# A trunk step of two layers: the first layer's modulation, made in the first stage or in part between the projections

## The reference, cut to what matters

```python
mod = silu(c) @ ada_w[l] + ada_b[l]              # 1024 x 6144: six vectors of 1024 for each group
sh1, sc1, g1, sh2, sc2, g2 = jnp.split(mod, 6, axis=-1)
h = _rms(x, norm1_g) * (1 + sc1) + sh1           # needs sh1 and sc1 alone
... = _split_in(h @ p['w_in'])                   # projections: q, k, v of four branches, gates
... four attentions, with head norms and rotary embedding; gates; w_out ...
x = x + g1 * y                                   # needs g1
h2 = _rms(x, norm2_g) * (1 + sc2) + sh2          # sc2, sh2
x = x + g2 * _peer(h2, ...)                      # g2; 16384 experts, top 16 of 8 heads
```

## Time and profile before

| | us |
|---|---|
| median of three timed runs (5416.52 to 5420.11) | 5418.61 |
| the profiled execution | 5413.07 |
| its span | 5411.3 |

### The profile page before, as it was taken

How to read it: one execution, slowest core, us unless ns; L and a number is a source line. 1 busy time by engine, 2 the same in 40 slices (tenths; PEclk the granted TensorE clock), 3 DMA queues, 4 the chain that set the end, 5 groups by cost and what they waited for, 6 DMA issues and landing times.

```text
span 5411.3 us, 68396 instructions
## 1 busy us (share of the span) xinstructions
PE 5099.5 (94%) x25512; PEld 4124.9 (76%) x25512; DVE 3206.5 (59%) x7229; ACT 1676.5 (31%) x2610; POOL 1325.4 (24%) x858
## 2 busy tenths in 40 slices
PE   4979999889999999999989799998899999999999
PEld 1846688677888887888868467877788888788887
DVE  1556411107998995666654763111488998766666
ACT  2325422222333332222232353212233333322222
POOL 1310022214344331111123001213244344211111
PEclk6978999999999999999999799999999999999999
DMA  6200021264877878888831001222367877888886
GB/s 228 71 29 1 11 73 65 74 242 170 270 239 260 281 258 308 289 288 291 293 121 58 15 1 35 68 65 66 131 219 263 280 261 239 316 286 294 291 288 222
DMA packets 349128, 981.98 MB, mean 181 GB/s; under 512 B 31648, under 2 KB 100128, under 8 KB 345504
## 3 DMA queue, kind: packets, MB, share of 16 engines
q1 hardware_dynamic: 215232, 553.19, 31.6%
q0 software_dynamic: 74880, 276.86, 14.6%
q10 hardware_dynamic: 58720, 148.04, 7.0%
HBM read 829.43 MB, written 148.54 MB: 181 GB/s over the span
## 4 chain that ended last, share of the span: by engine, by line
PE 84%; DVE 6%; DMA 3%; ACT 3%; POOL 1%; issue 1%; DVEq 1%; ACTq 0%; POOLq 0%; SPq 0%
PE PS L813 26%; PE PS L773 23%; PE PS L474 15%; PE PS L463 5%; PE PS L795 4%; PE PS L601 3%; PE PS L627 2%; PE PS L464 1%; DVE AR L1183 1%; PE PS L611 1%; POOL HR L1516 1%; PE PS L571 1%; DMA WR<-in_ada 1%; PE PS L761 1%; DVE SM L1222 1%
## 5 line engine op out<-in xcount | busy, mean ns | idle before, releaser
L813 PE MATMUL PS<-HB,VR 128*128 128x512 f32 x6144 | 1397.1, 390 | 17.2 <-DVE HB L1473 17.2
L813 PEld LDWEIGHTS PS<-HB,VR 128*128 128x128 f32 x6144 | 1156.3, 188 | 258.0 <-issue 18.0
L773 PE MATMUL PS<-HR,UR 128*128 128x512 f32 x4128 | 1013.0, 399 | 0.0
L1516 POOL TENSOR_TENSOR UR<-WR,UR 128x1024 fp32r<-128x1024 f32 x212 | 530.6, 2504 | 1838.7 <-ACT UR L995 938.0
L474 PE MATMUL PS<-HR,UR 128*128 128x320 f32 (+1 forms) x5952 | 924.0, 315 | 44.0 <-POOL HR L1516 38.8
L474 PEld LDWEIGHTS PS<-HR,UR 128*128 128x128 f32 x5952 | 888.4, 190 | 69.9 <-issue 47.6
L773 PEld LDWEIGHTS PS<-HR,UR 128*128 128x128 f32 x4128 | 768.2, 190 | 166.9
L1460 DVE TENSOR_TENSOR VR<-HT,VR 128x1024 fp32r<-128x1024 f32 x256 | 313.8, 1226 | 459.7 <-ACT VR L1113 374.4
L1113 ACT CAST VR<-HT 128x1024 fp32r<-128x1024 f32 x256 | 268.8, 1050 | 962.7 <-PE PS L813 960.2
L773 PE MATMUL PS<-HR 128*128 128x512 f32 x2016 | 486.7, 394 | 0.0
L773 PEld LDWEIGHTS PS<-HR 128*128 128x128 f32 x2016 | 372.1, 188 | 73.6
(11 more groups left out here) (183 smaller groups left out, 5975.4 us busy)
## 6 DMA issues: line engine op xcount, KB each, us to landing
WR<-in_uT SPq DMA_DIRECT2D x256, 512.0 KB
HT<-in_vtab SPq DMA_DIRECT2D x256, 512.0 KB, 4.0
activations<-AR ACTq DMA_DIRECT2D x256, 256.0 KB
gates_by_expert<-AR ACTq DMA_DIRECT2D x128, 512.0 KB, 3.5
HW<-activations SPq DMA_DIRECT2D x256, 256.0 KB
WR<-gates_by_expert SPq DMA_DIRECT2D x64, 1024.0 KB
WR<-in_wgate SPq DMA_DIRECT2D x64, 640.0 KB, 3.9
WR<-in_ada SPq DMA_DIRECT2D x24, 1024.0 KB, 4.9
```

What stands on the lines that cost most here:

```text
L773: last = pe.matmul(bank(n % 2), u_part(n, w)[:, c, :], HR[:, h, c, 0:LAT], start=c == 0 and i == 0, stop=c == DC - 1 and i == 2)
L813: last = pe.matmul(bank(d), VR[:, m % 4, w, P * d:P * d + P], HB[:, (m + 1) % 3, h, :], start=m == 0 and i == 0, stop=m == E1 - 1 and i == 2)
L1516: nc.gpsimd.tensor_tensor(dst, src, high.bitcast(F32), ALU.subtract).then_inc(sem_, 1)
```

## The change

The first stage of layer one keeps only the first third of the modulation, 8 steps of 24, and puts each behind one chunk of the norm's sums (`norm_sum`). The ring's numbers follow (`N_FIRST` = 16 blocks instead of 48). The other 16 steps (`rest_step`) run in stage two, two ahead of each of the projections 0 to 7, from two buffers of their own (REST_W, in space that the values and the keys of branch D fill later), and add up in PSUM bank 7. ScalarE copies the rows out at s = 3 and s = 7, TensorE turns them at s = 9, VectorE copies, adds the bias and makes the second scale at s = 10; `values` waits for that copy. GpSimd clears the row buffers at the start of stage two. SP issues the first four loads behind the first four projection blocks and the norm's sums, the others behind blocks 4 to 9. In stage one VectorE now takes the reciprocal before it waits for the turned modulation. Layer two is as before.

```diff
-B_FM = N_ADA
+N_FIRST = N_ADA // SETS
+B_FM = N_FIRST
...
+        REST_W = [VT[:, 0:4, :].rearrange("p a b -> p (a b)"), DKF[:, 0:2 * D]]
+        REST_R = [VT[:, 5, :], DKF[:, 2 * D:2 * D + 512]]
...
@@ SP
-                    with sp.Fori(0, N_ADA // RING) as i:
+                    with sp.Fori(0, N_FIRST // RING) as i:
...
+                def load_rest(step):
+                    if step >= 2:
+                        sp.wait_ge(rest_used, step - 1)
+                    sp.dma_start(REST_W[step % 2].rearrange("p (a t) -> p a t", a=2),
+                                 ada[l, N_FIRST + 2 * step:N_FIRST + 2 * step + 2].rearrange("a b t -> b a t")
+                                 ).then_inc(rest_in[step % 2], 16)
                 for n in range(RING):
                     load(l, B_FM + n, WR[:, (B_FM + n) % RING, 0:D], wfm[l, n])
+                if l == 0:
+                    sp.wait_ge(ss_ready, 1)
+                    for step in range(4):
+                        load_rest(step)
                 sp.wait_ge(hr_ready, l * (2 * DC) + DC)
...
                 for n in range(RING, N_FM):
                     load(l, B_FM + n, WR[:, (B_FM + n) % RING, 0:D], wfm[l, n])
+                    if l == 0 and 2 * n - 3 < 2 * DC:
+                        for step in (2 * n - 4, 2 * n - 3):
+                            load_rest(step)
@@ TensorE
+            def norm_sum(c):
+                pe.wait_ge(sq_ready, c + 1)
+                last = both(cols(0), ones, lambda lo, hi: NSQ[:, c, lo:hi], c == 0, c == DC - 1)
+                if c == DC - 1:
+                    last.then_inc(ss_ready, 1)
...
             def values(l):
                 pe.wait_ge(y_ready, l * NI + N_FM)
+                pe.wait_ge(rest_kept, 1)
...
+                def rest_step(step):
+                    which, c = divmod(step, DC)
+                    pe.wait_ge(rest_in[step % 2], 16 * (step // 2 + 1))
+                    if step == DC:
+                        pe.wait_ge(rest_out, 1)
+                    for j in range(4):
+                        last = pe.matmul(bank(7)[32 * j:32 * j + 2, :], CS[:, 2 * c:2 * c + 2],
+                                         REST_W[step % 2][:, 512 * j:512 * j + 512], start=c == 0, stop=c == DC - 1)
+                    last.then_inc(rest_used, 1)
+
+                def turn_rest():
+                    pe.wait_ge(rest_out, 2)
...
+                    for which in range(2):
+                        for q in range(4):
+                            last = pe.matmul(out[:, which, :, q, :], REST_R[which][:, P * q:P * q + P], pick, start=True, stop=True)
+                    last.then_inc(rest_turned, 1)
-                norm(l, 0)
                 if l == 0:
-                    for which in range(SETS):
-                        for c in range(DC):
-                            modulation(which, c)
-                    for which in range(SETS):
-                        turn_modulation(which)
+                    for c in range(DC):
+                        norm_sum(c)
+                        modulation(0, c)
+                    turn_modulation(0)
+                else:
+                    norm(l, 0)
                 phase_end(pe, l, 0)
                 for s in range(NI + 2):
+                    if l == 0 and s < DC:
+                        rest_step(2 * s)
+                        rest_step(2 * s + 1)
+                    if l == 0 and s == 9:
+                        turn_rest()
@@ ScalarE
+            def rest_rows(which):
+                act.wait_ge(rest_used, DC * (which + 1))
...
+                for j in range(4):
+                    rows = slice(32 * j, 32 * j + 2)
+                    last = nc.scalar.copy(REST_R[which][rows, :], bank(7)[rows, :])
+                last.then_inc(rest_out, 1)
...
-                    for which in range(SETS):
-                        modulation_rows(l, which)
+                    modulation_rows(l, 0)
...
                 for s in range(NI + 1):
+                    if l == 0 and s in (3, 7):
+                        rest_rows(s // 4)
@@ VectorE
                 if l == 0:
-                    dve.wait_ge(ada_turned, SETS)
-                    nc.vector.tensor_copy(NEXT[:, :], MODT)
+                    norm(l, 0)
+                    dve.wait_ge(ada_turned, 1)
+                    nc.vector.tensor_copy(NEXT[:, 0:32], MODT[:, 0:32])
...
                 for s in range(1, NI + 2):
+                    if l == 0 and s == 10:
+                        dve.wait_ge(rest_turned, 1)
+                        nc.vector.tensor_copy(NEXT[:, 32:96], PF[:, 3584:3648]).then_inc(rest_kept, 1)
+                        dve.drain()
+                        nc.vector.tensor_tensor(MD[:, 32:96], NEXT[:, 32:96], GN[:, G_ADAB + 32:G_ADAB + 96], ALU.add)
+                        dve.drain()
+                        nc.vector.scalar_tensor_tensor(SC[:, 1], MD4[:, 4], 1.0, GN[:, G_N2:G_N2 + 16].rearrange("p (c g) -> p c g", c=DC),
+                                                       ALU.add, ALU.mult)
@@ GpSimd
+                if l == 0:
+                    nc.gpsimd.memset(REST_R[0], 0.0)
+                    nc.gpsimd.memset(REST_R[1], 0.0).then_inc(rest_clear, 1)
                 low_h(0)
```

More of the change, by code:

```diff
@@ L69, in loads @@
 def loads(l, n):
-    first = N_ADA if l else 0
-    pairs = 0 if l else sum(m % RING == n % RING for m in range(N_ADA) if m < n)
+    first = N_FIRST if l else 0
+    pairs = 0 if l else sum(m % RING == n % RING for m in range(N_FIRST) if m < n)
     before = loads(l - 1, BLOCKS + n % RING) if l else 0
@@ L78, in block_no @@
 def block_no(l, n):
-    return l * (BLOCKS - N_ADA) + n
+    return l * (BLOCKS - N_FIRST) + n
 SPLIT_NO = {n: i for i, n in enumerate([*range(B_FM, B_DQ), *range(B_GATE, B_WOUT), *range(B_WQ, BLOCKS)])}
@@ L215, in build @@
         shared = a.at
+        DKF = DK.rearrange("p a b -> p (a b)")
+        REST_W = [VT[:, 0:4, :].rearrange("p a b -> p (a b)"), DKF[:, 0:2 * D]]
+        REST_R = [VT[:, 5, :], DKF[:, 2 * D:2 * D + 512]]
         q_ = Arena(AR, shared, AF)
@@ L293, in build @@
         cs_sig = sem("cs_sig")
+        rest_in, rest_used = [sem(f"rest_of_modulation_in{k}") for k in range(2)], sem("rest_of_modulation_used")
+        rest_clear, rest_out, rest_turned, rest_kept = (sem(n) for n in (
+            "rest_rows_cleared", "rest_rows_out", "rest_turned", "rest_kept"))
         next_in, next_used = [sem(f"next_modulation_in{k}") for k in range(3)], sem("next_modulation_used")
@@ L651, in turn_modulation @@
                     last.then_inc(ada_turned, 1)
-                norm(l, 0)
-                if l == 0:
-                    for which in range(SETS):
-                        for c in range(DC):
-                            modulation(which, c)
-                    for which in range(SETS):
-                        turn_modulation(which)
+                def rest_step(step):
[9 more added lines that the diff above has]
+                    pe.wait_ge(rest_out, 2)
+                    out = PF[:, 3584:3648].rearrange("p (s j q g) -> p s j q g", s=2, j=4, q=4)
+                    pick = ident.rearrange("p (j r) -> p j r", j=4)[:, :, 0:2]
+                    for which in range(2):
+                        for q in range(4):
+                            last = pe.matmul(out[:, which, :, q, :], REST_R[which][:, P * q:P * q + P], pick, start=True, stop=True)
+                    last.then_inc(rest_turned, 1)
+                if l == 0:
+                    for c in range(DC):
[4 more added lines that the diff above has]
+                    norm(l, 0)
                 phase_end(pe, l, 0)
                 for s in range(NI + 2):
+                    if l == 0 and s < DC:
[3 more added lines that the diff above has]
+                        turn_rest()
                     if s == N_FM:
@@ L929, in modulation_rows @@
                 last.then_inc(ada_out, 1)
+            def rest_rows(which):
+                act.wait_ge(rest_used, DC * (which + 1))
+                if which == 0:
+                    act.wait_ge(rest_clear, 1)
+                for j in range(4):
+                    rows = slice(32 * j, 32 * j + 2)
+                    last = nc.scalar.copy(REST_R[which][rows, :], bank(7)[rows, :])
+                last.then_inc(rest_out, 1)
             def heads(l, g):
@@ L1287, in _ @@
                 if l == 0:
-                    dve.wait_ge(ada_turned, SETS)
-                    nc.vector.tensor_copy(NEXT[:, :], MODT)
+                    norm(l, 0)
+                    dve.wait_ge(ada_turned, 1)
+                    nc.vector.tensor_copy(NEXT[:, 0:32], MODT[:, 0:32])
                     dve.drain()
-                nc.vector.tensor_tensor(MD[:, :], NEXT[:, :], GN[:, G_ADAB:G_ADAB + 2 * N_ADA], ALU.add)
+                made = 32 if l == 0 else 2 * N_ADA
+                nc.vector.tensor_tensor(MD[:, 0:made], NEXT[:, 0:made], GN[:, G_ADAB:G_ADAB + made], ALU.add)
                 dve.drain()
```

(5 more changed lines are left out.)

## The result

The changed kernel took 5368.31 us (median of four runs, 5360.51 to 5376.23) against 5417.68 us for the kernel before (5416.52 to 5420.11): the ratio is 0.991, interval 0.9897 to 0.9924. It is faster by 49 us, where 56 were forecast (5362.5), and lies inside the stated range of 5356 to 5376. The profiled execution took 5360.51 us, its span 5358.7 against 5411.3 us: 52.6 us less, where 56.1 were forecast.

A forecast was written before the change was run, and what follows sets the result against it. TensorE was 84% of the chain, DMA 3%, with layer one's first stage at the DMA's pace. −71.3 + 2.6 + 10.2 + 1.75 + 0.7 = −56.1 us gave 5362.5 us; range 5356 to 5376 for 8 in 10.

The forecast's parts named there:

- Stage one: Layer one's first stage, left with 8 of 24 steps, ends at 47.6 us instead of 118.95: 71.3 us saved.
- rival (a): In stage one TensorE sets the pace at the low clock, ending it 6.8 us later: 5369 us; chance 12%.
- Steps 0 and 1, the clears: Ahead of projection 0, two moved steps and GpSimd's two new clears fit in idle time: cost 0.
- Steps 2 to 5: Ahead of projections 1 and 2, four moved steps with a stall for step 5: 2.6 us, bounds 1.1 to 4.
- Five pairs: Ahead of projections 3 to 7, two moved steps each on a full TensorE at 2.03 us a pair: 10.2 us.
- The turn: At step 9 of stage two, TensorE's 8 products that turn the rows: 1.75 us, bounds 1.75 to 3.5.
- VectorE's three instructions: Copy, addition, product at step 10; the product, held beside GpSimd's subtraction, makes the chain 0.7 us late; bounds 0 to 0.8.
- The sum: Whole kernel: all terms together give −56.1 us, a median of 5362.5 us; chance 68%, bounds 5358 to 5371.
- (b): In the projections, moved loads are late, seven pairs waiting 0.5 to 2 us each: about 5371 us; chance 15%.
- (c): Ahead of projections, no landing is hidden and moved steps stall TensorE: up to 5440 us; 3% together with (d).
- (d): In the projections, waits drop TensorE to the low clock, fourteen costing 59 us: 5421 us; 3% together with (c).
- signs of failure: Waits for moved loads over 3 us, stage one's barrier after 52 us, or a later stage changing over 2 us.

The follow-up runs named there:

- e8: The changed kernel with the norm's eight sums ahead of the eight modulation steps instead of between them: 5379.2 us, ratio 0.9941 to the kernel before.
- e1: The changed kernel run and profiled again with no edit: 5370.5 us, ratio 0.9917 to the kernel before.
- e3: The changed kernel with VectorE's bias addition and second scale moved from s = 10 to the stage's end: 5359.4 us, ratio 0.9895 to the kernel before.
- e5: The kernel before, run and profiled again with no edit: 5420.6 us against 5408.3 in the same group, ratio 1.0016.

## Why the prediction was right, and where its terms were off

- *Stage one, −71.3.* Measured −70.8 (118.98 to 48.18). The mechanism held: the DMA's round, forecast at 5.95 us per slot pair, was 6.3 (22.53 to 28.84), the clock stayed up, and rival (a) is ruled out by the clock of 1.00. e8 splits it: 9.1 us come from putting the steps between the sums, with the clock that this keeps up, the rest from the sixteen steps taken out. GpSimd ended the stage as said, but not alone: VectorE's last product (L1363) took 2.20 us beside GpSimd's subtraction and ended with it, at 48.05.
- *Steps 0 and 1, the clears: 0.* Right. Step 1 waited 0.60 us in TensorE's idle time, the clears took 0.53 us each while GpSimd had nothing to do.
- *Steps 2 to 5, +2.6 with bounds 1.1 to 4.* This term was too small: +4.3 in e1, +7.0 in the first profile. The loads for steps 4 and 5 landed at 80.5 and 83.0, 32.3 and 34.8 us after the barrier, where the forecast has 30.5 and 33.1; and the wait for step 4 was not in it. The cause is a misread row: the block ahead of them was put at 141.24 + 5.5, the median of two blocks, where it had landed at 141.24 + 7.4. With 7.4 the same sum lands the two loads 32.3 and 34.9 us after the barrier, as measured, and gives some +4.5. What such waits do to the clock was not priced at all: 0 to 2.7 us, by the execution. The part on GpSimd's subtraction was right (L1256 took 0.34 us in the first profile and 0.35 in e1).
- *Five pairs, +10.2.* The period is 11.01, as said (11.1). But the period of the kernel before to compare it with is not 9.1 for the first of the five: it was 10.65, since its own wait of 2.75 us had cost it the clock (that projection took 9.18 us). So five pairs cost 55.03 − 46.98 = 8.05 us. This error of 2.1 us hid the 1.7 of the term before: luck.
- *The turn, +1.75.* Measured 1.73 (period 10.83 against 9.10).
- *VectorE's three instructions, +0.7 with bounds 0 to 0.8.* This is the term that was furthest off. The right mechanism was named, one product held by one subtraction. But the addition has two SBUF operands as well and was held first (2.38 us), the product was then held by GpSimd's next instruction (1.13), and the late chain met a third (L1270, 2.36), after which TensorE fell to the low clock. e3 prices it all at 6.0 us.
- *The sum.* Up to the values +15.25 forecast, +20.3 in e1: 1.7 more, 2.1 less, 5.3 more and 0.1 of rest. With 0.5 less in stage one and 0.4 in the other stages, that is 50.1 us between e1 and e5 instead of 56.1. The gain is right in kind and 6 us too large. Of the range, the lower end does not follow from its reason: without the stall and without VectorE's delay the sum gives 5360, not 5356.
- *Rivals.* (b) was half right: late loads, but for two steps and not for seven pairs; from step 6 on no step waited. (c) and (d) did not occur. Of the forecast's own signs of failure, a later stage that changes by over 2 us occurred, and e5 shows that it was a poor sign: the kernel before does so by itself. The waits for the moved loads, with 3 us as the limit, are at it: 1.42 + 1.44 = 2.86 us for steps 4 and 5, and 3.46 with step 1's 0.60, which cost nothing.
- *The rules.* On the switch of tiling the row stands (11.01 is 9.05 + 1.96, and 1.90 of it are the products). The limit of the Trainium skill's "DMA: Bandwidth & Descriptors", section Specifications, would have landed step 5's load 1.4 us later than I had it (an estimate; the prediction's 1.3 is a slip: 4.7 MB take 13.1 us at 358 GB/s and 11.75 at 400). It landed 1.7 us later, but by the misread row and not by that limit: while it came, the rate was 419 GB/s, above it. The Trainium skill's "SBUF — State Buffer", section SBUF: two separate sides, says that VectorE with two SBUF inputs and GpSimd reading SBUF take turns for whole instructions. The trace agrees in these cases: 2.38, 1.13, 2.36 and 2.43 us with two SBUF operands beside GpSimd, 0.69 with one of them in PSUM, and GpSimd's clears at 0.53 beside VectorE's scaling. Applied to all three new instructions, it would have said that the addition is held too. The kernel before showed it as well: the product that makes the scales in its stage one (L1295) took 2.15 us beside GpSimd's subtraction.

## What to carry to other kernels

Work of a DMA-bound first stage can be moved under a compute-bound one at the price of its products, if its loads are ahead by more than the burst that they queue in: here 16 MB of loads cost 11 us of products and turn (1.2 + 8.1 + 1.7), and 3 to 6 us for the one place where they queued behind tables. A row that gives the median of two transfers is not the time of the first: take each by itself. A small VectorE instruction on two SBUF operands can last as long as what GpSimd is doing at that moment (2.38 us for 64 columns); place it where nothing follows, as in e3. That feeding it from PSUM avoids this is shown here for the rotation's product, not for the addition itself. Before a stage is credited with a gain, profile the unchanged kernel twice: here whole stages have two or more lengths.

## What the runs showed of the hardware that was not expected

A stretch of the same instructions has different lengths, which go with TensorE's granted clock: in the fourteen profiles layer one's tail takes 109.8 to 112.6 or 117.5 us (clock 0.82 to 0.85, and 0.77 at 117.5), its attention 262 to 273 (0.89 to 0.84), its gates 388.0, 389.7 or 392.1 to 392.8 (0.99 to 0.98). Two executions with waits of 1.42 + 1.44 and of 1.50 + 1.43 us at the same place had a clock that fell (0.78 from 79 to 85 us, first block below) and one that did not (1.00, second block); three others lie between. What decides it is not shown.

```profile
79.00:85.00 6.00, 3.14 (x18) 0.39 (x18) 2.42 (x1) 3.44 (x5) 2.36 (x1) 0.78 0.98 359
```

```profile
79.00:85.00 6.00, 3.07 (x24) 1.21 (x24) 2.47 (x1) 3.40 (x5) 2.35 (x1) 1.00 0.96 358
```
